# A fused two-layer encoder kernel: sums by ones for two small products, a third rounded weight tile, and a new order at the last chunks

## What is computed

```python
xn = rms_norm(x, pre_norm[layer]);  proj = xn @ w_in[layer]
ya = dilated_attention(...) * silu(a_gate)
yb = banded_window_attention(..., sink) * silu(b_gate)
yc = hgrn2_bidirectional(c_q, c_ff, c_fb, c_i, c_gate, lb, hgrn_norm)
y = g0*(ya @ w_branch_a) + g1*(yb @ w_branch_b) + g2*(yc @ w_branch_c)
x = x + rms_norm(y @ w_out[layer], post_norm[layer])
```

## Time and profile before

| | |
|---|---|
| median of 3 runs | 2173.27 us (2173.22 to 2173.32) |
| the profiled execution | 2173.16 us, of which its span is 2171.3 us |
| busy in the span | PE 2162.0, DVE 1479.4, POOL 1287.3, ACT 1063.6 us |
| matmuls recorded | 10094 |
| HBM traffic | 401.99 MB at 185 GB/s |

### The profile page before, as it was taken

The page is one execution under the profiler, slowest core; times in us unless marked ns, Lnnn a source line. Parts: engine busy times, 40 slices in busy tenths (PEclk is TensorE's granted clock), DMA queues, the critical chain, the costliest instruction groups (busy, mean ns, idle before and its releaser), DMA issues.

```text
span 2171.3 us, 25793 instructions
## 1 busy us (share of the span) xinstructions
PE 2162.0 (100%) x10094; PEld 1807.8 (83%) x10094; DVE 1479.4 (68%) x2131; ACT 1063.6 (49%) x1042; POOL 1287.3 (59%) x583
## 2 busy tenths in 40 slices
PE   9999999999999999999999999999999999999998
PEld 7888888888888888888878888888888888888887
DVE  7872789878656785554378637898796566865633
ACT  5434344546556554434454434345466566544443
POOL 4455544446685767666544555444576857676664
PEclk9999999999999999999999999999999999999999
DMA  8555455355444444655555554454444444546554
GB/s 322 193 193 193 172 175 184 146 176 184 167 172 176 174 175 174 252 193 187 186 213 195 192 193 175 168 181 150 181 176 175 174 174 165 185 170 250 193 186 151
DMA packets 59752, 403.66 MB, mean 186 GB/s; under 512 B 6768, under 2 KB 6896, under 8 KB 12272
## 3 DMA queue, kind: packets, MB, share of 16 engines
q1 hardware_dynamic: 59488, 401.49, 51.4%
q10 hardware_dynamic: 144, 0.52, 0.1%
HBM read 397.80 MB, written 4.19 MB: 185 GB/s over the span
## 4 chain that ended last, share of the span: by engine, by line
PE 98%; DMA 1%; ACT 0%; issue 0%; POOL 0%; DVE 0%; DVEq 0%; POOLq 0%; ACTq 0%
PE acc L1248 91%; PE side L1248 6%; DMA raw<-w_stream 1%; PE side L1423 0%; ACT w_hi L468 0%; PE side L413 0%; ACT xT_hi L422 0%; DVE w_lo L471 0%; POOL w_lo L471 0%; PE side L1470 0%; DVE arena L886 0%; POOL small L569 0%; ACT stage L634 0%; DVEq L483 0%; ACT w_hi L678 0%
## 5 line engine op out<-in xcount | busy, mean ns | idle before, releaser
L471 POOL TENSOR_TENSOR w_lo<-raw,w_hi 128x768 fp32r<-128x768 f32 x367 | 1064.1, 2899 | 848.9 <-ACT w_hi L468 837.9
L468 ACT ACTIVATE w_hi<-raw 128x2048 fp32r<-128x2048 f32 x365 | 699.1, 1915 | 983.9 <-PE acc L1248 976.4
L471 DVE TENSOR_TENSOR w_lo<-raw,w_hi 128x1280 fp32r<-128x1280 f32 (+1 forms) x373 | 585.8, 1572 | 595.3 <-ACT w_hi L468 592.9
L1248 PE MATMUL acc<-w_hi,xT_hi 128*128 128x512 f32 x2112 | 654.4, 393 | 0.7 <-ACT w_hi L468 0.7
L1248 PE MATMUL acc<-w_hi,xT_lo 128*128 128x512 f32 x2112 | 647.8, 389 | 0.0
L1248 PE MATMUL acc<-w_lo,xT_hi 128*128 128x512 f32 x2112 | 528.3, 392 | 0.3 <-DVE w_lo L471 0.2
L1248 PEld LDWEIGHTS acc<-w_hi,xT_lo 128*128 128x128 f32 x2112 | 396.5, 188 | 83.5 <-DVE xT_lo L432 0.2
L1248 PEld LDWEIGHTS acc<-w_hi,xT_hi 128*128 128x128 f32 x2112 | 392.5, 188 | 80.4 <-ACT w_hi L468 1.6
L1248 PEld LDWEIGHTS acc<-w_lo,xT_hi 128*128 128x128 f32 x2112 | 392.2, 188 | 79.8 <-DVE w_lo L471 1.2
L923 DVE STREAM_TRANSPOSE arena<-stage 32x256 f32<-32x256 f32 (+1 forms) x480 | 204.9, 427 | 7.1
L1248 PEld LDWEIGHTS side<-arena 128*128 128x128 f32 x864 | 118.6, 191 | 9.9
(11 more groups left out here) (151 smaller groups left out, 1908.2 us busy)
## 6 DMA issues: line engine op xcount, KB each, us to landing
raw<-w_stream SPq DMA_DIRECT2D x366, 1024.0 KB, 4.8
x_out<-arena SPq DMA_DIRECT2D x16, 256.0 KB, 2.6
arena<-x_turned_in SPq DMA_DIRECT2D x4, 514.0 KB, 7.4
arena<-x_in SPq DMA_DIRECT2D x2, 1024.0 KB, 14.6
arena<-x_in SPq DMA_DIRECT2D x4, 512.0 KB, 5.7
wide<-post_in SPq DMA_DIRECT2D x2, 1024.0 KB, 7.0
arena<-x_out SPq DMA_DIRECT2D x4, 512.0 KB, 5.7
raw<-w_stream SPq DMA_DIRECT2D x3, 512.0 KB, 7.1
```

The source lines that it names most:

```text
L468: return act.activation(w_hi[:, g % 2, :], raw[:, g % LANDING, :], ACT.Copy)
L471: return eng.tensor_tensor(w_lo[:, g % LANDING, cols], raw[:, g % LANDING, cols], w_hi[:, g % 2, cols].bitcast(F32), ALU.subtract)
L1248: return pe.matmul(out, a, b, start=start, stop=stop)
```

## The change

- `w_hi` has three tiles. ACT may round tile g once step g-3 is over; in step s ACT, DVE and POOL prepare tile s+2. The piecewise preparation at the seam goes.
- The products n=0 and n=1 of a unit are no longer matmuls of keys with queries. DVE multiplies keys and queries element by element (for n=1 with the two tokens of a pair crossed), ACT rounds the 128x512 result (`products_hi`), DVE writes the remainder (`products_lo`), and PE sums over channels by two matmuls 128x512 with a left side of ones. DVE takes n=0 with the identity as factor. Product n=1 is issued in the step of level 1, ahead of n=2, and kept one step later.
- ACT clips the logarithms (as a Relu) and scales q in d=3, in place of DVE in d=2 and d=4.
- The steps of chunks 49 and 50 are put in another order: quarters 0 to 2 of both, then the last quarter of both. y's last quarter is transposed by DVE like the others, and not by PE. Chunk 49 ends at step 174 and is scaled one step after, not two.
- At the start tile 3 goes ahead of x's first half, tile 4 ahead of x's second half, and the masks behind tile 5. ACT's order is square, tile 4, square, tile 5; POOL does tile 5's part ahead of the power.

```diff
@@ steps
+STEPS[STEP_OF[OUT0]:STEP_OF[OUT0 + 2]] = [(OUT0 + i, q) for i in range(2) for q in range(3)] + [(OUT0, 3), (OUT0 + 1, 3)]
@@ ACT, rounding
-                    if g >= 2:
-                        act.wait_ge(pe_step, g - 1)
+                    if g >= ROUNDED:
+                        act.wait_ge(pe_step, g - ROUNDED + 1)
@@ POOL, loop
-                        g = layer * NSTEPS + s + 1
-                        if s < NSTEPS - 1:
+                        g = layer * NSTEPS + s + 2
+                        if s < NSTEPS - 1 and g < TOTAL:
                             lo(g)
@@ SP, start
+                weights(3)
                 x_of(0)
-                weights(3)
-                x_of(1)
@@ ACT, d == 3
+                                act.activation(rec_views(u)[1], PI, ACT.Relu, bias=neg_ln_tiny, scale=-1.0)
+                                for h in range(2):
+                                    v = rec_views(u)[0][:, h * T:(h + 1) * T]
+                                    ins = act.activation(v, v, ACT.Copy, scale=one_lb[:, head + h:head + h + 1])
+                                ins.then_inc(S.q_scaled, 1)
@@ ACT, d == 5
+                                act.wait_ge(S.paired, 2 * u + 1)
+                                act.activation(products_hi, EQ[:, 1], ACT.Copy).then_inc(S.pair_hi, 1)
@@ ACT, level 1
+                                        act.wait_ge(S.paired, 2 * u + 2)
+                                        act.wait_ge(S.grams, (LEVELS + 1) * u + 1)
+                                        act.activation(products_hi, EQ[:, 3], ACT.Copy).then_inc(S.pair_hi, 1)
@@ DVE, d == 2 and 4
-                                dve.tensor_scalar(z, PI, LN_TINY, 0.0, ALU.add, ALU.min).then_inc(S.rec_prep, 1)
-                                for h in range(2):
-                                    cols = slice(h * T, (h + 1) * T)
-                                    dve.tensor_scalar(q[:, cols], q[:, cols], one_lb[:, head + h:head + h + 1], None, ALU.mult)
+                                dve.wait_ge(S.q_scaled, u + 1)
+                                dve.tensor_tensor(keys(-1), keys(-1), q, ALU.mult).then_inc(S.paired, 1)
@@ DVE, d == 5
+                                dve.wait_ge(S.pair_hi, 2 * u + 1)
+                                dve.tensor_tensor(products_lo, keys(-1), products_hi.bitcast(F32),
+                                                  ALU.subtract).then_inc(S.pair_lo, 1)
@@ DVE, levels
+                                for n in {0: [0], 1: [], 2: [1, 2]}.get(l, [l]):
+                                if l == 1:
+                                    dve.wait_ge(S.pair_hi, 2 * u + 2)
+                                    dve.tensor_tensor(products_lo, EQ[:, 3], products_hi.bitcast(F32),
+                                                      ALU.subtract).then_inc(S.pair_lo, 1)
                                 dve.wait_ge(S.decays, LEVELS * u + l + 1)
                                 dve.tensor_tensor(EQ[:, 3], q, EQ[:, 0], ALU.mult).then_inc(S.mixed, 1)
+                                if l == 0:
+                                    dve.wait_ge(S.mixed, LEVELS * u + 1)
+                                    dve.tensor_tensor(crossed(EQ[:, 3], 0, 1, 0), crossed(EQ[:, 3], 0, 1, 0),
+                                                      crossed(keys(0), 1, -1, 0), ALU.mult).then_inc(S.paired, 1)
@@ PE, level_grams
+                        if l <= 0:
+                            pe.wait_ge(S.pair_hi, 2 * u + l + 2)
+                            mm(dst, ones[:, :], products_hi, stop=False)
+                            pe.wait_ge(S.pair_lo, 2 * u + l + 2)
+                            mm(dst, ones[:, :], products_lo, start=False).then_inc(S.grams, 1)
+                            continue
@@ PE, y's last quarter
-                            for i in range(blocks):
-                                for m in range(MT):
-                                    ins = pe.transpose(ps[:, i * T + m * P:i * T + (m + 1) * P],
-                                                       src[:, m, i * P:(i + 1) * P], ident)
```

More of the change, by code:

```diff
@@ L79 @@
 NSTEPS = len(STEPS)
[L80 to L82 removed]
+OUT0 = len(CHUNKS) - 4
+STEPS[STEP_OF[OUT0]:STEP_OF[OUT0 + 2]] = [(OUT0 + i, q) for i in range(2) for q in range(3)] + [(OUT0, 3), (OUT0 + 1, 3)]
+ENDS = {_s: _c for _s, (_c, _q) in enumerate(STEPS) if _q == CHUNKS[_c][2] // QK - 1}
 def end_of(kind, i):
@@ L110 @@
 LANDING = 4
+ROUNDED = 3
 assert NSTEPS % LANDING == 0
@@ L186, in build @@
         warm = sb("warm", [P, P])
+        ones = sb("ones", [P, P], F32R)
         def piece(at, shape, dt=F32):
@@ L221, in build @@
         q_tanh = piece(64, [4, T])
+        ropes = piece(72, [2, MT * 4 * ROT])
         c_turned = probsT[:, 0:2 * T].rearrange("p (h t) -> p h t", t=T)
@@ L314, in build @@
                           yT_lo[:, 4 * j:4 * j + 4, :], None,
-                          side[1][:, :] if j == 3 else flat(y_turned)))
+                          flat(y_turned)))
         TURN_AT = {t[0]: n for n, t in enumerate(turns)}
-        BY_BLOCKS = range(len(turns) - 1)
         def split_at(s):
-            n = TURN_AT.get(s - 1)
-            m = TURN_AT.get(s - 2)
-            return m if m in BY_BLOCKS else n if n not in BY_BLOCKS else None
+            return TURN_AT.get(s - 2)
         def lhs(c, k):
@@ L523, in _ @@
                         if layer == 0 and s == 0:
+                            x_of(1)
+                        if layer == 0 and s == 1:
                             sp.dma_start(y[:, 0, 0:MT * MASK_COLS], MASKS).then_inc(masks_landed, 16)
+                        if layer == 0 and s == 2:
                             sp.dma_start(y[:, 1, 0:(LEVELS - 1) * P], LMASKS).then_inc(masks_landed, 16)
@@ L576, in _ @@
                     for s in range(NSTEPS):
-                        g = layer * NSTEPS + s + 1
-                        if s < NSTEPS - 1:
+                        if layer == 0 and s == 0:
+                            lo(1)
+                        g = layer * NSTEPS + s + 2
+                        if s < NSTEPS - 1 and g < TOTAL:
                             lo(g)
@@ L617, in _ @@
                         if m == 0 and layer + 1 < DEPTH:
-                            lo((layer + 1) * NSTEPS)
+                            lo((layer + 1) * NSTEPS + 1)
             @block.scalar
@@ L848, in _ @@
                     if layer + 1 < DEPTH:
-                        hi((layer + 1) * NSTEPS)
+                        hi((layer + 1) * NSTEPS + 1)
                     else:
@@ L873, in out_scaled, with out_chunk @@
                                              post_gain[:, i * CW:(i + 1) * CW], ALU.mult)
+                def out_chunk(layer, i):
+                    S = of_layer[layer]
+                    dve.wait_ge(S.branch_turned, 8 + i)
+                    for m in range(MT):
+                        dve.wait_ge(S.out_squared, 2 * i + m + 1)
+                        ins = out_scaled(layer, i, m)
+                    ins.then_inc((S.acc_free0, S.acc_free1)[(OUT0 + i) % 2], 1)
                 def out_sum(S, m):
@@ L950, in _ @@
                 dve.memset(warm[:, :], 0.0).then_inc(warm_ready, 1)
+                dve.wait_ge(warm_ready, 1)
+                dve.tensor_scalar(ones[:, :], warm[:, :], 0.0, 1.0, ALU.mult, ALU.add)
                 for layer in range(DEPTH):
@@ L999, in _ @@
                         lo(g + 3)
+                        lo(g + 4)
                     for s in range(3, NSTEPS):
-                        if s < NSTEPS - 1:
-                            lo(layer * NSTEPS + s + 1)
+                        if s < NSTEPS - 1 and layer * NSTEPS + s + 2 < TOTAL:
+                            lo(layer * NSTEPS + s + 2)
                         if s == 3:
@@ L1269, in hi_pass @@
                         pe.wait_ge(hi_ready, g)
-                    if layer and s == 1:
-                        pe.wait_ge(S.half_hi, 1)
                     for t, n in order:
@@ L1288, in lo_pass @@
                     c, q = STEPS[s]
-                    in_pieces = layer and s == 1
-                    if g and not in_pieces:
+                    if g:
                         pe.wait_ge(lo_dve, g)
@@ L1355, in last_two_steps, with grams_of, level_grams @@
                         renewed(layer + 1, 1)
-                def level_grams(s):
+                def grams_of(s):
                     for u in range(4):
                         l = s - 1 - REC[u] - FIRST_LEVEL
-                        if not -1 <= l < LEVELS:
-                            continue
-                        q = rec_views(u)[0]
+                        for level in {0: [], 1: [0, 1]}.get(l, [l] if -1 <= l < LEVELS else []):
+                            yield u, level
+                def level_grams(s):
+                    for u, l in grams_of(s):
                         n = (LEVELS + 1) * u + l + 1
-                        pe.wait_ge(S.mixed, n + 1)
                         if n >= 2:
@@ L1521, in stream_of @@
```

(3 more changed lines are left out.)

123 lines of the change are left out of this document (53 added, 70 removed).

## The result

The changed kernel takes 2208.08 us (median of 5 runs, 2207.45 to 2209.26) against 2173.32 (2173.22 to 2173.66). The ratio is 1.0161, with a 95% interval of 1.0149 to 1.0172. It is 1.6% slower, where the prediction had 2165.0 and a chance of 0.03 for slower.

A forecast was written before the change was run, and what follows sets the result against it. PE was taken as the bound, busy 2162.0 of 2171.3 us. Terms -7.2 - 1.8 - 1.1 + 0.4 + 1.4 = -8.3 us gave 2173.3 - 8.3 = 2165.0 us, range 2161.3 to 2169.

The forecast's parts named there:

- Units 1 to 3 have no transposes beside them; 0 there: In the recurrence's units 1 to 3, PE was expected to lose nothing to new waits: 0 us.
- the +1.4 for the recurrence: PE waits 0.7 us at level 2 of unit 0, once per layer: +1.4 us, between 0 and +4.
- no more in sum: DVE loses the clip and two scalings, gets four 128x512 operations of 0.67 us each if undisturbed: no more work.
- The rule that I weighed: Four new DVE operations per unit can each hold POOL up to 0.67 us; the third tile's 5.44 us covers it.
- The start (e): Start: first two tile waits go, but sorting matmuls wait for POOL's factors; +0.4 us, bounds -1.3 and +1.5.
- (a): Recurrence: two products per unit become two 512-column matmuls each, saving 0.46 us per product; 7.2 us taken, range 5.7 to 7.3.
- (b): Last quarter of y: eight PE transposes per layer go to DVE, saving 0.88 us x 2 layers = 1.8 us.
- (c): New order of chunks 49 and 50: accumulator read within step 175 with 0.7 us margin; no wait, 0 us taken.
- (d): Seam: the loss at tile 1's remainder goes as tile 1 is rounded earlier; -1.1 us, between -0.6 and -1.7.
- The rival of the handovers in every unit: New DVE, ACT, DVE, PE chains cost each of 8 units 0.8 us more: 2171.4 us, chance 0.10.
- The rival of POOL as the pace of the levels: POOL slows to 7.5 us per step in the levels, costing 28 us: 2193 us, chance 0.03.
- The sentence on what would prove it wrong: Wrong if all units wait for new rounding or remainder, PE for w_lo in the levels, or chunk 51 for its accumulator.

The follow-up runs named there:

- experiment 1: Changed kernel with the recurrence as before (both products by matmuls in own steps, clips and scales on DVE): 2173.78 us, ratio 1.0004.
- Experiment 2: Changed kernel with ACT's logarithm ahead of its wait for the paired factor and the rounding in step d=5: 2192.97 us.
- experiment 10: experiment 7 with DVE's rest of the product with itself moved behind the logs of d=6: 2174.86 us.
- experiment 12: Changed kernel with logarithm first, rest of the product with itself behind the logs, factors first; both sums by ones, clips on ACT: 2190.76 us.
- Experiments 13: experiment 11 with DVE's rest of the product left out, PE taking the rounded product twice: 2166.04 us, ratio 0.9968.
- experiment 14: experiment 11 with the product's rest on POOL, behind its remainder of d=5: 2166.23 us, ratio 0.9967.
- experiment 11: experiment 10 with clips and scales back on DVE, so only the product with itself is a sum by ones in the recurrence: 2174.61 us.
- experiments 2, 3: Changed kernel with the clip of the logarithm's input and the scaling of q back on DVE: 2198.62 us.
- 8: Changed kernel with the logarithm ahead of the rounding and clips and scales on DVE, both products by ones: 2191.45 us.
- experiment 9: experiment 1 with the factors and sorting matrix ahead of tile 5 in both layers: 2168.04 us, ratio 0.9976.
- experiment 7: Changed kernel with logarithm first, the pair's product by matmuls in its own step, and factors and sorting matrix ahead of tile 5: 2173.47 us.

## Why the prediction was wrong

**The step that failed: "Units 1 to 3 have no transposes beside them; 0 there", and with it the +1.4 for the recurrence.** By experiment 1 the recurrence cost 34.3 us in all; the sums saved 6.4 of their own (below), so the waits and their half clock, which the sum had at 1.4, were about 41. The units 1 and 3, put at 0, lost 3.4 and 8.2 us in layer 0. Three things were missed:

- *ACT's queue in d=5.* I counted ACT's rounding as 0.6 us of work. It is a wait as well: the logarithm, which every level needs, is queued behind it, and ACT stands 2.4 to 3.8 us ahead of it, waiting for DVE's product. Experiment 2 gives 15.1 us back by order alone, in the units 1 and 3.
- *The pair's handover.* The prediction saw it in unit 0 and put it at 0.7 us; ACT's rounding began 4 us after the product was ready. Between experiments 10 and 12 it costs 15.9 us, where it was meant to gain 0.45 us per unit.
- *DVE's one more instruction.* I took "no more in sum" from counts at 0.67 us each, but from experiment 1 to the changed kernel DVE's busy time rises by 52 us (1500.9 to 1552.8). The rest took 0.68 us alone and 2.3 each time that POOL's remainder had begun ahead of it. Experiments 13 and 14 give the price of the first product's rest: 8.6 and 8.4 us for eight instructions.

The rule that I weighed (the Trainium skill, SBUF — State Buffer, section "SBUF: two separate sides": whichever of DVE's two-input operation and POOL's starts first holds the shared ports for the whole instruction) speaks of the same thing. I applied it to POOL, as the one held up. The rows agree with it the other way round: L1072 at 2.34 instead of 0.68 where POOL had begun 0.22 us ahead (experiment 11), L1081 at 4.59 for two instead of 1.40. And they agree with its "starts first": where L1072 began ahead of POOL's remainder, it kept its 0.68.

These prices aren't a sum. The runs take one thing out at a time, the parts overlap (experiments 2, 3 and 8), and a collision of DVE with POOL in one step moves the next.

**Half clock.** The sum had no term for it. It made 13 of the 34.8 us of the profiled execution. No rival had it either.

**The start (e)**: +0.4 forecast, +3.95 measured. Tile 5 landed by 29.72 (forecast 29.3), and POOL's remainder ended at 33.56, inside the forecast. The factors then took 2.5 us in place of 1.2 (L571 took 1.31 beside DVE's remainder, where 0.2 was taken), so they came at 36.06 (34.3 to 35.5). The failed part is whom PE waits for, 1.2 us longer still: DVE's queue was not followed, where the lower bounds and the sorting matrix also stand behind tile 5's remainder now.

**Right:** (a), the price of a product by ones: 516.44 - 516.21 = 0.23 us a matmul (experiment 14), and 0.40 saved per product, where 0.45 was taken (step table, experiment 14, units 0 and 1), so 16 x 0.40 = 6.4 us in place of 7.2. (b): 0.90 us in layer 0 (experiment 9, steps 134 to 170), as forecast. (c): nothing waits, steps 170 to 183 gain 0.2. (d): -1.4 at the seam against -1.1.

The rival of the handovers in every unit had one of the right mechanisms, with a price of 0.8 us per unit. With the price that experiment 12 gives, 16 us for the pair alone, it ends on the other side; and this loss is in the first and last units, not in every one. The rival of POOL as the pace of the levels did not come: PE's waits name DVE and ACT. But POOL's remainder had its part, as what held DVE up. The sentence on what would prove it wrong, waits for the new rounding or remainder, names what came, in the units 0, 1 and 3. The 0.03 for slower was far too little.

## What to carry to other kernels

An instruction added to an in-order engine costs what stands behind it, so follow each queue from the new wait to the next thing that the bounding engine needs; half a microsecond of work cost 15 us here, and the same instruction three lines lower did not. Where an operation takes one time alone and another beside a neighbour's, price it at the longer one and look for the engine that is idle at that moment. A saving and a loss bundled in one change can be parted: the seam, the output and the product with itself by ones, with the factors and the logarithm first, the clips back on DVE and the rest on POOL, make 2165.5 to 2166.2 out of a kernel of 2208, and 2173.3 before.

## What was not expected of the hardware

A wait of PE was followed by work at a granted clock of 0.53 (537 to 543 us, the 1.2 GHz level) although PE was busy again, so a wait cost more than its length: 13 us of half clock came on top of 28 us of waits. Before, PE did no work at half clock (mean 0.999). In experiment 14, with no wait over a microsecond in the recurrence, the mean is 0.999 again. Short waits were enough: in experiment 7 PE's longest wait in the recurrence was 1.9 us, once in each layer, and both were followed by such a stretch; in experiment 10 it was 1.4 us, and none followed.

Which of DVE and POOL begins first decides who pays. The same instruction took 0.68 or 2.34 us by a shift of 0.35 us between the two engines (0.22 behind POOL's remainder or 0.13 ahead of it, experiment 11).
